# A gated unit that starts on the unnormalised state: two tiles in quarters, the deviation multiplied in at the evacuations

## The chip, the cores and the metric

The kernel runs as one program on one core of a Trainium2 chip. The metric is the device time of one execution in microseconds (us), the median of several runs. The engines run their own instruction streams and wait for each other by semaphores: TensorE (matmuls, weights 128x128, up to 512 columns a matmul, sums in eight PSUM banks), VectorE (DVE), ScalarE (ACT, with function tables), GpSimd (POOL) and SyncE, which here issues the weight loads.

## What is computed

Two transformer blocks over 256 positions and a width of 2048, all in f32. The change concerns the end of the first block, its gated unit:

```python
h = h + mixed @ w_out[l]

v = rms_norm(h, norm_ffn[l])
h = h + (jax.nn.silu(v @ w_ffn_gate[l]) * (v @ w_ffn_up[l])) @ w_ffn_down[l]

def rms_norm(x, g):
    xf = x.astype(jnp.float32)
    y = xf * lax.rsqrt(jnp.mean(xf * xf, axis=-1, keepdims=True) + RMS_EPS)
    return (y * g.astype(jnp.float32)).astype(x.dtype)
```

`w_ffn_gate` and `w_ffn_up` are 2048 x 5632. The norm's factor (one over the deviation) is one number for each position, so it is the same for all rows of a product's input and can be multiplied into the product instead.

## The kernel before

The state is kept transposed: `hT` holds 16 blocks (`KC`) of 128 features by 256 positions (`T`). An f32 product is made of three matmuls in the fast format f32r: every weight and every activation is split into a high and a low part, and high x high, high x low and low x high are summed in PSUM. A **tile** is 128 output features: 1 MB of weights, 48 matmuls of 256 columns, in two **halves** (units) of 24.

Weights come by SyncE into a ring `raw` of four tiles. `half()` exists on two engines: ScalarE copies half a tile to its high part `wh` (L1104), VectorE subtracts it from `raw` to get the low part `wl` (L1728). `wh` and `wl` have four slots, one for a half each. ScalarE may write a slot when TensorE has begun the unit behind the one that used it (semaphore `begun`, counted by `begin`). The order in each engine's stream is written out by hand. A `half()` placed before or after another step says when it can run.

`tile_T` (L510) makes one tile: 16 high x high and high x low matmuls in turn (L519, L520), then 8 with the low weights (L527), twice. It names the bank, and `reserve` lets TensorE wait until the bank's reader has freed it (`free_v6` is bank 6, read by VectorE). The names `xh`, `xl` are the split activations; in the profile both read `x`.

The steps around the change are these. `residual("out", KC)` runs 16 rows of the out projection (L578, L580, L585) into all eight banks, then VectorE adds the banks to `hT` (L1770), two banks a flag `h_ready`. ScalarE squares `hT` by quarters into `tmp` (L1181), TensorE sums the squares over partitions with 16 matmuls against ones (`sum_squares`, L607), VectorE makes the variance (L1778), ScalarE the root (L1183), VectorE the reciprocal (L1782) and four products a quarter (L1793). ScalarE splits off the high part (L1188) and VectorE the low part (L1787). `awake_till_std` runs 56 filler matmuls meanwhile (L502). Then the gated unit: for 22 turns, gate tile, up tile, gate tile, up tile, in banks 0, 4, 1, 5. ScalarE applies Silu to the gate bank (L1374), VectorE multiplies with the up bank into `hidT` (L2110).

After the norm VectorE raises `masks_free`, for which GpSimd waits to build the masks of the second block (L2667, L2627).

Of the kernel before, what the change touches and what calls it, by code (L numbers as in the profile page):

```python
# [170 lines left out]
def hold(eng, sem, value):  # L171
# [7 lines left out]
    "PE ffn": {"full_a0": 1, "begun": 8, "full_a1": 1, "full_v4": 1, "full_v5": 1},  # L179
# [7 lines left out]
    "ACT ffn": {"hi": 8, "got land0": 1, "got land1": 1, "got land2": 1, "got land3": 1, "free_a1": 1, "free_a0": 1, "gate_ready": 2},  # L187
# [7 lines left out]
    "DVE ffn": {"lo": 8, "got land0": 1, "got land1": 1, "got land2": 1, "got land3": 1, "got gate_ready": 2, "free_v4": 1, "free_v5": 1},  # L195
# [9 lines left out]
def build(nc, dram, out):  # L205
# [4 lines left out]
    with ctx:  # L210
        S = {}

        def sem(*keys):
            for key in keys:
                S[key] = ctx.enter_context(nc.semaphore(key))
# [12 lines left out]
        sem("sq_added", "gains_ready", "spread", "a_ready", "gg_in", "rs_done", "nq_ready")  # L228
# [107 lines left out]
        gt2 = at("gt2", 48, [P, 2, T])  # L336
        memT = at("memT", 32, [P, KC, T])
# [117 lines left out]
        def _(pe):  # L455
# [341 lines left out]

            residual("out", KC)
            sum_squares()
            awake_till_std(2, xkh[:, 0, :])  # L800
            normed_x()
            marks["ffn"] = k.n["full_v4"], k.n["full_v5"]
            for f in range(2):
                reserve(4 + f)
                tile_T(f, spare=None if f else 7)
                tile_T(4 + f, "v")
            with k.loop("ffn", pe, FT // 2 - 1):
                for f in range(2):
                    reserve(4 + f)
                    tile_T(f)  # L810
                    tile_T(4 + f, "v")
# [267 lines left out]
        def _(act):  # L1079
# [300 lines left out]
            with k.loop("ffn", act, FT // 2 - 1) as i:  # L1380
                unit_turn(i)
            unit_turn(FT // 2 - 1, True)
# [316 lines left out]
        def _(dve):  # L1699
# [31 lines left out]
            def split(width=HW):  # L1731

                half()
                half(width)
# [12 lines left out]
            def residual(src, name, n, more=True, between=None, early=False):  # L1747
                flag("src_ready")
                if not early:
                    for j in range(2):  # L1750
                        xsplit(src, j)
                if between is not None:
                    for j in range(n - 4):
                        split()
                        xsplit(src, 2 + j)
                        between(j)
                elif n > 4:
                    with k.loop(name, dve, n // 4 - 1) as i:
                        for j in range(4):
                            split()  # L1760
                            xsplit(src, i * 4 + (2 + j))
                for j in range(2):
                    split()
                    xsplit(src, n - 2 + j)
                if more:
                    split()
                for b in range(8):
                    take(b)
                    h = hT[:, 2 * b:2 * b + 2, :]
                    v.tensor_tensor(h, h, ps[:, b, :].rearrange("p (a t) -> p a t", a=2),  # L1770
                                    ALU.add).then_inc(*k.up(f"free_v{b}"))
                    if b % 2:
                        flag("h_ready")

# [320 lines left out]
            residual(mix1, "out", KC, early=True)  # L2095
            flag("masks_free")
            norm(hT, "norm_ffn")
            split()
            def unit_turn(i, last=False):

                for n in range(2):
                    split()
                    half()
                    if last and n == 1:
                        early_rows(hidT)
                    else:
                        half()
                    dve.wait_ge(*k.next("gate_ready"))
# [7 lines left out]
            with k.loop("ffn", dve, FT // 2 - 1) as i:  # L2116
                unit_turn(i)
            flag("early_ready")
            unit_turn(FT // 2 - 1, True)
# [682 lines left out]
```

## Time and profile before

| | |
|---|---|
| median of 3 runs (lowest, highest) | 4031.9 us (4029.94, 4036.97) |
| the profiled execution | 4031.73 us, its span 4030.0 us |
| TensorE busy, VectorE, ScalarE, GpSimd | 3969.0, 2380.7, 2064.1, 61.1 us |
| mean granted TensorE clock | 0.998 of 2.4 GHz |
| out projection ends, gated unit's first matmul | 820.78, 835.50 us |
| bytes read from HBM | 712.5 MB, 179 GB/s over the span |

All numbers of the profile come from one execution on the chip. A matmul's duration in it is longer than its share of the engine's time, because matmuls are pipelined; the distance from one start to the next is what counts. Idle times of an engine are listed with the instruction that ended them.

### The profile page before, as it was taken

How to read it: one execution, taken by the hardware profiler on the slowest of the kernel's cores; microseconds unless marked ns; L12 is line 12 of the kernel's file. 1: busy time of each engine (PE TensorE's matmuls, PEld its weight loads, DVE VectorE, ACT ScalarE, POOL GpSimd, SP SyncE). 2: the span in 40 equal slices, each digit the busy share in tenths (PEclk: the TensorE clock that was granted, in tenths of full speed). 3: DMA queues.
4: the chain of work that ended last, by engine and by line, in shares of the span. 5: the costliest groups of instructions: out<-in, count | busy, mean ns of one | idle time of the engine just before them, and what ended most of it. 6: DMA issues, size and time to landing. Idle time of an engine off the chain costs nothing.

```text
span 4030.0 us, 82891 instructions
## 1 busy us (share of the span) xinstructions
PE 3969.0 (98%) x34070; PEld 3923.8 (97%) x34070; DVE 2380.7 (59%) x3435; ACT 2064.1 (51%) x3120; POOL 61.1 (2%) x71
## 2 busy tenths in 40 slices
PE   8999999999999999999999999999999999999998
PEld 8999999999999999999999999999999999999998
DVE  7655565554444556544665666997765555555555
ACT  7555554455555444445554454447754444444443
POOL 1000000000000000000000000000000000000000
PEclk9999999999999999999999999999999999999999
DMA  5445555545555555443335544554555556665553
GB/s 209 178 158 178 179 176 186 193 157 191 194 193 193 190 195 183 168 159 125 147 137 178 178 157 147 189 190 177 183 195 197 189 194 214 217 209 193 191 195 128
DMA packets 111190, 726.10 MB, mean 180 GB/s; under 512 B 11296, under 2 KB 11424, under 8 KB 29184
## 3 DMA queue, kind: packets, MB, share of 16 engines
q1 hardware_dynamic: 105904, 701.55, 49.0%
q0 software_dynamic: 5072, 21.50, 1.7%
q8 instruction: 159, 2.61, 0.3%
q14 instruction: 55, 0.45, 0.0%
HBM read 712.52 MB, written 10.49 MB: 179 GB/s over the span
## 4 chain that ended last, share of the span: by engine, by line
PE 94%; DVE 3%; ACT 2%; issue 1%; DMA 0%; DVEq 0%; SPq 0%; ACTq 0%
PE ps L519 19%; PE ps L527 19%; PE ps L520 19%; PE ps L578 9%; PE ps L585 9%; PE ps L580 9%; PE ps L1041 1%; PE ps L651 1%; PE ps L548 1%; PE ps L549 1%; PE ps L550 1%; DVE wl L1728 1%; ACT wh L1104 1%; PE ps L607 1%; PE ps L669 1%
## 5 line engine op out<-in xcount | busy, mean ns | idle before, releaser
L1728 DVE TENSOR_TENSOR wl<-raw,wh 128x1024 fp32r<-128x1024 f32 x1328 | 1622.6, 1230 | 1446.1 <-ACT wh L1104 1440.8
L1104 ACT ACTIVATE wh<-raw 128x1024 fp32r<-128x1024 f32 x1328 | 1402.2, 1060 | 1735.5 <-PE ps L578 603.6
L519 PE MATMUL ps<-x,wh 128*128 128x256 f32 x6656 | 1582.7, 280 | 10.2 <-DVE x L1787 5.1
L520 PE MATMUL ps<-x,wh 128*128 128x256 f32 x6656 | 1567.6, 278 | 0.0
L519 PEld LDWEIGHTS ps<-x,wh 128*128 128x128 f32 x6656 | 1254.3, 188 | 19.1 <-issue 10.2
L520 PEld LDWEIGHTS ps<-x,wh 128*128 128x128 f32 x6656 | 1254.2, 188 | 0.5
L527 PE MATMUL ps<-x,wl 128*128 128x256 f32 x6656 | 899.3, 278 | 0.3 <-DVE wl L1728 0.3
L527 PEld LDWEIGHTS ps<-x,wl 128*128 128x128 f32 x6656 | 825.1, 188 | 0.5 <-DVE wl L1728 0.5
L578 PE MATMUL ps<-xkh,wh 128*128 128x256 f32 x3328 | 776.5, 276 | 3.0 <-DVE xkl L1739 1.8
L580 PE MATMUL ps<-xkl,wh 128*128 128x256 f32 x3328 | 775.7, 276 | 0.0
L578 PEld LDWEIGHTS ps<-xkh,wh 128*128 128x128 f32 x3328 | 624.8, 188 | 4.7 <-DVE xkl L1739 2.8
L580 PEld LDWEIGHTS ps<-xkl,wh 128*128 128x128 f32 x3328 | 624.8, 188 | 0.0
L585 PE MATMUL ps<-xkh,wl 128*128 128x256 f32 x3328 | 444.9, 276 | 0.0
L585 PEld LDWEIGHTS ps<-xkh,wl 128*128 128x128 f32 x3328 | 408.2, 188 | 0.0
L548 PE MATMUL ps<-y,wh 128*128 128x256 f32 x448 | 125.9, 281 | 0.0
L549 PE MATMUL ps<-y,wh 128*128 128x256 f32 x448 | 124.7, 278 | 0.0
L550 PE MATMUL ps<-y,wl 128*128 128x256 f32 x448 | 124.6, 278 | 0.0
L1635 ACT ACTIVATE oh_g<-oh_g,g_t 128x128 f32<-128x128 f32 x256 | 81.8, 390 | 9.3 <-DVE oh_g L2530 8.5
L548 PEld LDWEIGHTS ps<-y,wh 128*128 128x128 f32 x448 | 84.8, 189 | 0.7 <-issue 0.7
L550 PEld LDWEIGHTS ps<-y,wl 128*128 128x128 f32 x448 | 84.2, 188 | 0.0
L549 PEld LDWEIGHTS ps<-y,wh 128*128 128x128 f32 x448 | 84.1, 188 | 0.0
L519 PE MATMUL ps<-y,wh 128*128 128x256 f32 x192 | 48.5, 292 | 15.7 <-ACT wh L1104 15.0
(378 smaller groups left out, 2412.2 us busy)
## 6 DMA issues: line engine op xcount, KB each, us to landing
raw<-in_w_in SPq DMA_DIRECT2D x184, 1024.0 KB, 4.8
raw<-in_expert_u SPq DMA_DIRECT2D x128, 1024.0 KB, 4.8
raw<-in_expert_v SPq DMA_DIRECT2D x128, 1024.0 KB, 4.7
raw<-in_w_ffn_gate SPq DMA_DIRECT2D x44, 1024.0 KB, 4.7
raw<-in_w_ffn_up SPq DMA_DIRECT2D x44, 1024.0 KB, 4.7
raw<-in_w_ffn_down SPq DMA_DIRECT2D x44, 1024.0 KB, 4.7
raw<-in_w_out SPq DMA_DIRECT2D x32, 1024.0 KB, 4.7
raw<-in_w_branch SPq DMA_DIRECT2D x16, 1024.0 KB, 4.9
```

The lines of the kernel that those rows point to most:

```text
L519: begin(mm(o, wh[:, j, c], x_h[:, kc, :], start=kc == 0, stop=False), kc % 8 == 0)
L520: mm(o, wh[:, j, c], x_l[:, kc, :], start=False, stop=False)
L527: m = mm(o, wl[:, j, c], x_h[:, kc, :], start=False, stop=kc == KC - 1)
L548: begin(mm(o, wh[:, j, c], yh[:, y0 + n, :], start=n == 0, stop=False), kc % 8 == 0)
L549: mm(o, wh[:, j, c], yl[:, y0 + n, :], start=False, stop=False)
L550: m = mm(o, wl[:, j, c], yh[:, y0 + n, :], start=False, stop=n == nk - 1)
L578: begin(mm(o, wh[:, j, c], xkh[:, x, :], start=first and t % 2 == 0, stop=False, skip_group_check=True), t % 8 == 0)
L580: mm(o, wh[:, j, c], xkl[:, x, :], start=False, stop=False, skip_group_check=True)
L585: m = mm(o, wl[:, j, c], xkh[:, x, :], start=False, stop=last, skip_group_check=True)
L1104: f(wh[:, u % 4, 0:width], raw[:, ring, c:c + width], ACT.Copy).then_inc(*k.up("hi"))
L1635: f(o, o, ACT.Copy, scale=g_t[:, 4 * n + s:4 * n + s + 1]).then_inc(*k.up("act" if s < 3 else "lr_ready"))
L1728: v.tensor_tensor(wl[:, u % 4, 0:width], raw[:, ring, c:c + width], wh[:, u % 4, 0:width].bitcast(F32), ALU.subtract).then_inc(*k.up("lo"))
```

## The change

The gated unit takes `hT` times the gain `norm_ffn`, without the division by the deviation. ScalarE makes the high parts straight from `hT` as each quarter is ready (`raw_high`), VectorE the low parts (`raw_low`). TensorE runs the first gate tile and the first up tile together (`raw_pair`, banks 2 and 6): quarter by quarter all matmuls on high activations, then all matmuls on low activations. All four slots of `wh` and `wl` hold their weights meanwhile. The second pair of tiles follows in banks 3 and 7. VectorE adds the squares from 16 blocks down to 4, and TensorE sums them with 4 matmuls behind the fourth tile. Every evacuation then multiplies by the reciprocal `rstd`: VectorE writes the scaled gate to `gs` (Silu reads it there) and the scaled up tile to `hidT`, and multiplies the two in place. The fillers, the normalised products and their splits are gone. Loops on ScalarE and VectorE have one turn less, since the first pairs stand ahead of them.

```diff
 # TensorE
+            def raw_pair(banks, readers):
+                reserve(*banks)
+                base = k.at("begun")
+                slot = [(k.n["begun"] + u) % 4 for u in range(4)]
+                for q in range(4):
+                    pe.wait_ge(*k.next("raw_hi"))
+                    for t, b in enumerate(banks):
+                        u = 2 * t + q // 2
+                        if q % 2 == 0:
+                            pe.wait_ge(S["hi"], base + u + 1)
+                            pe.wait_ge(S["lo"], base + u + 1)
+                        for kc in range(4 * q, 4 * q + 4):
+                            c = slice(kc % 8 * P, (kc % 8 + 1) * P)
+                            begin(mm(reg(b), wh[:, slot[u], c], xh[:, kc, :], start=kc == 0, stop=False), kc == 0 and t == 0)
+                            mm(reg(b), wl[:, slot[u], c], xh[:, kc, :], start=False, stop=False)
+                for q in range(4):
+                    pe.wait_ge(*k.next("raw_lo"))
+                    for t, b in enumerate(banks):
+                        u = 2 * t + q // 2
+                        for kc in range(4 * q, 4 * q + 4):
+                            c = slice(kc % 8 * P, (kc % 8 + 1) * P)
+                            m = mm(reg(b), wh[:, slot[u], c], xl[:, kc, :], start=False, stop=kc == KC - 1)
+                            begin(m, (t, kc) in ((0, 8), (1, 12), (1, 13)))
...
             residual("out", KC)
-            sum_squares()
-            awake_till_std(2, xkh[:, 0, :])
-            normed_x()
             marks["ffn"] = k.n["full_v4"], k.n["full_v5"]
-            for f in range(2):
-                reserve(4 + f)
-                tile_T(f, spare=None if f else 7)
-                tile_T(4 + f, "v")
+            raw_pair((2, 6), "vv")
+            tile_T(3, "v", spare=0)
+            tile_T(7, "v")
+            sum_added(1, 1)
 # ScalarE
             residual(mix1, "out", KC, early=True)
-            norm(hT)
-            split(True)
+            half()
+            raw_high("norm_ffn", 0)
+            raw_high("norm_ffn", 1)
+            half()
+            raw_high("norm_ffn", 2)
+            raw_high("norm_ffn", 3)
+            for q in range(3):
+                squares(q)
+            half()
+            squares(3)
+            for _ in range(6):
+                half()
...
             def unit_turn(i, last=False):
                 for n in range(2):
-                    done(n)
-                    f(gt2[:, n, :], ps[:, n, 0:T], ACT.Silu).then_inc(*k.up(f"free_a{n}"))
-                    flag("gate_ready")
+                    half()
+                    act.wait_ge(*k.next("scaled"))
+                    half(True)
+                    silu(n)
 # VectorE
-            residual(mix1, "out", KC, early=True)
+            residual(mix1, "out", KC, early=True, halves=(3, 7))
+            for q in range(4):
+                raw_low("norm_ffn", q)
             flag("masks_free")
-            norm(hT, "norm_ffn")
-            split()
+            for _ in range(3):
+                half()
+            add_squares(8)
+            for _ in range(4):
+                half()
+            take(1)
...
             def unit_turn(i, last=False):
                 for n in range(2):
-                    split()
+                    half()
+                    scaled(n, gs[:, n, :])
+                    flag("scaled")
+                    half()
                     half()
...
+                    hid = dyn(hidT, i * 2 + (n + 2))
+                    scaled(4 + n, hid)
+                    own()
                     dve.wait_ge(*k.next("gate_ready"))
-                    take(4 + n)
-                    v.tensor_tensor(dyn(hidT, i * 2 + n), ps[:, 4 + n, 0:T], gt2[:, n, :],
-                                    ALU.mult).then_inc(*k.up(f"free_v{4 + n}"))
+                    v.tensor_tensor(hid, hid, gt2[:, n, :], ALU.mult).then_inc(*k.up("dve"))
```

TensorE before, from the end of the out projection (L585) over the sum (L607) and the fillers (L502) to the first tile (L519). What an instruction waits for stands in brackets:

```order
L585 MATMUL ps<-xkh,wl 128x256 [waits lo]
L585 MATMUL ps<-xkh,wl 128x256 x7
L607 MATMUL ps<-tmp,ones 128x256 [waits sq_ready,free_v0,free_a0]
L607 MATMUL ps<-tmp,ones 128x256 x3
L607 MATMUL ps<-tmp,ones 128x256 [waits sq_ready]
L607 MATMUL ps<-tmp,ones 128x256 x3
...
L502 MATMUL ps<-xkh 128x256 [waits free_v7,free_a7]
L502 MATMUL ps<-xkh 128x256 x7
L502 MATMUL ps<-xkh 128x256 [waits rs_std]
L502 MATMUL ps<-xkh 128x256 x47
L519 MATMUL ps<-x,wh 128x256 [waits hi,free_v0,xl_ready,free_v4,free_a4]
```

TensorE after, the same place: L586 ends the projection, L813 and L814 are high activations with high and low weights, L821 the low activations, L520 the third tile.

```order
L586 MATMUL ps<-xkh,wl 128x256 x7
L813 MATMUL ps<-x,wh 128x256 [waits raw_hi,hi,free_v6,lo,free_v2,free_a2]
L814 MATMUL ps<-x,wl 128x256
...
L813 MATMUL ps<-x,wh 128x256 [waits lo,hi]
...
L813 MATMUL ps<-x,wh 128x256 [waits raw_hi]
...
L821 MATMUL ps<-x,wh 128x256 [waits raw_lo]
L821 MATMUL ps<-x,wh 128x256 x7
L821 MATMUL ps<-x,wh 128x256 [waits raw_lo]
L821 MATMUL ps<-x,wh 128x256 x7
...
L520 MATMUL ps<-x,wh 128x256 [waits hi,free_v3,free_a3]
L521 MATMUL ps<-x,wh 128x256
```

The sum and the fillers have gone from between the projection and the tiles. The first matmul waits for six semaphores, `free_v6` among them, and the low activations stand together at the pair's end.

VectorE before, the last adds into `hT` (L1770), the flags (L1713), the variance (L1778) and the reciprocal (L1782):

```order
L1770 TENSOR_TENSOR hT<-hT,ps 128x512 [waits full_v2]
L1770 TENSOR_TENSOR hT<-hT,ps 128x512 [waits full_v3]
L1713 MEMSET small 128x1 [waits free_v3]
L1770 TENSOR_TENSOR hT<-hT,ps 128x512 [waits full_v4]
...
L1770 TENSOR_TENSOR hT<-hT,ps 128x512 [waits full_v6]
L1770 TENSOR_TENSOR hT<-hT,ps 128x512 [waits full_v7]
L1713 MEMSET small 128x1 [waits free_v7]
L1713 MEMSET small 128x1 [waits h_ready]
L1778 TENSOR_SCALAR rstd<-ps 128x256 [waits full_v0]
L1713 MEMSET small 128x1 [waits free_v0]
L1782 RECIPROCAL rstd<-rstd 128x256 [waits rs_std]
```

VectorE after. L1837 are the adds, L1795 the low parts of weight halves, L1780 the flags, L2168 the low activations; the second MEMSET shown alone is `masks_free`.

```order
L1837 TENSOR_TENSOR hT<-hT,ps 128x512 [waits full_v3]
L1780 MEMSET small 128x1 [waits free_v3]
L1795 TENSOR_TENSOR wl<-raw,wh 128x1024 [waits hi,land3]
L1837 TENSOR_TENSOR hT<-hT,ps 128x512 [waits full_v4]
L1837 TENSOR_TENSOR hT<-hT,ps 128x512 [waits full_v5]
...
L1837 TENSOR_TENSOR hT<-hT,ps 128x512 [waits full_v6]
L1837 TENSOR_TENSOR hT<-hT,ps 128x512 [waits full_v7]
L1780 MEMSET small 128x1 [waits free_v7]
L1795 TENSOR_TENSOR wl<-raw,wh 128x1024 [waits hi]
L2168 SCALAR_TENSOR_TENSOR x<-hT,par,x 128x256 [waits raw_hi]
...
L1780 MEMSET small 128x1 [waits raw_lo]
L1795 TENSOR_TENSOR wl<-raw,wh 128x1024 [waits hi,land0]
```

One weight half has moved between the adds of banks 3 and 4, another behind bank 7, and the flag `masks_free` from behind the adds to behind the 16 low activations.

## Rows read from the trace of the kernel before

**Rows 1.** The page: busy us (share of the span) xinstructions, by engine.

```profile
PE 3969.0 (98%) x34070; PEld 3923.8 (97%) x34070; DVE 2380.7 (59%) x3435; ACT 2064.1 (51%) x3120; POOL 61.1 (2%) x71
```

**Rows 2.** TensorE's waits: line <- releaser: us in total, times, longest us.

```profile
PE ps L519 <- DVE x L1787: 5.1, 5, 1.6
```

**Rows 3.** TensorE's timeline around the change: start us, us, line, operation, shapes, count.

```profile
815.33 0.28 PE L578 MATMUL ps<-xkh,wh 128*128 128x256 f32 x1
...
820.78 7.07 PE L607 MATMUL ps<-tmp,ones 128*128 128x256 f32 x32
827.50 7.45 PE L502 MATMUL ps<-xkh 128*128 128x256 f32 x56
835.50 0.36 PE L519 MATMUL ps<-x,wh 128*128 128x256 f32 x1 [0.56 <-DVE x L1787]
...
843.34 0.33 PE L496 MATMUL ps<-x,wh 128*128 128x384 f32 x1
843.51 1.07 PE L527 MATMUL ps<-x,wl 128*128 128x256 f32 x8
...
857.12 1.07 PE L527 MATMUL ps<-x,wl 128*128 128x256 f32 x8
...
859.84 1.07 PE L527 MATMUL ps<-x,wl 128*128 128x256 f32 x8
```

**Rows 4.** Two windows: length, busy us of each engine, TensorE clock, DMA share, GB/s.

```profile
823.90:835.50 11.60, 10.90 (x75) 10.06 (x74) 6.95 (x15) 4.26 (x5) 4.20 (x8) 1.00 0.00 0
870.00:1310.00 440.00, 440.00 (x3885) 440.00 (x3884) 212.26 (x204) 239.34 (x281) 0.00 (x0) 1.00 0.54 193
```

**Rows 5.** VectorE's timeline: the program's start, then around the change.

```profile
8.65 6.42 DVE L1840 SCALAR_TENSOR_TENSOR y<-hT,par,y 128x256 fp32r<-128x256 f32 x16 [8.65 <-POOL rstd L2656]
...
821.12 1.41 DVE L1770 TENSOR_TENSOR hT<-hT,ps 128x512 f32<-128x512 f32 x2
...
827.88 0.42 DVE L1778 TENSOR_SCALAR rstd<-ps 128x256 f32<-128x256 f32 x1 [4.50 <-PE ps L607]
...
834.14 1.22 DVE L1787 TENSOR_TENSOR x<-tmp,x 128x1024 fp32r<-128x1024 f32 x1
...
842.18 2.35 DVE L1728 TENSOR_TENSOR wl<-raw,wh 128x1024 fp32r<-128x1024 f32 x2
```

**Rows 6.** ScalarE's timeline: the program's start, then around the change.

```profile
7.50 6.49 ACT L1223 ACTIVATE y<-hT,par 128x256 fp32r<-128x256 f32 x16
...
815.64 1.06 ACT L1104 ACTIVATE wh<-raw 128x1024 fp32r<-128x1024 f32 x1 [1.60 <-PE ps L578]
...
821.96 1.06 ACT L1181 ACTIVATE tmp<-hT 128x1024 f32<-128x1024 f32 x1 [0.26 <-DVE small L1713]
```

**Rows 7.** VectorE: a sum of 2048 columns by shape (mean ns), and two halves at 59 us.

```profile
L1823 DVE TENSOR_TENSOR pr<-pr,rinv 128x2048 f32<-128x2048 f32 x8 | 18.3, 2292 | 0.3
...
59.21 4.55 DVE L1728 TENSOR_TENSOR wl<-raw,wh 128x1024 fp32r<-128x1024 f32 x2
```

**Rows 8.** GpSimd's timeline.

```profile
59.36 3.32 POOL L2662 TENSOR_TENSOR nq<-hT,rstd 128x1024 f32<-128x1024 f32 x1 [1.15 <-DVE x L1905]
823.46 0.56 POOL L2667 IOTA nd<- 128x512 f32 x1 [760.78 <-DVE small L1713]
824.17 0.62 POOL L2627 TENSOR_SCALAR_AFFINE_SELECT nd<-nd 128x512 f32<-128x512 f32 x1
```

**Rows 9.** TensorE at the norm of a later stage, and windows as in rows 4.

```profile
2449.07 0.36 PE L519 MATMUL ps<-x,wh 128*128 128x256 f32 x1 [0.55 <-DVE x L1787]
...
2451.83 0.58 PE L519 MATMUL ps<-x,wh 128*128 128x256 f32 x1 [1.59 <-DVE x L1787]
...
1860.00:1880.00 20.00, 19.76 (x144) 19.35 (x143) 4.40 (x7) 7.46 (x12) 0.00 (x0) 0.83 0.29 100
2440.00:2460.00 20.00, 17.71 (x129) 16.99 (x128) 17.59 (x31) 8.84 (x10) 0.00 (x0) 0.91 0.05 8
2452.00:2454.00 2.00, 2.00 (x10) 2.00 (x11) 1.96 (x6) 0.48 (x1) 0.00 (x0) 0.50 0.00 0
```

More of the change, by code:

```diff
@@ L1378, in unit_turn @@
                     done_v(4 + n, i + (marks["ffn"][n] + 1))
-            with k.loop("ffn", act, FT // 2 - 1) as i:
+            with k.loop("ffn", act, FT // 2 - 2) as i:
                 unit_turn(i)
-            unit_turn(FT // 2 - 1, True)
+            unit_turn(FT // 2 - 2, True)
             residual(hidT, "down", FT, early=True)
@@ L1745, in early_rows, with residual @@
                     xsplit(src, j)
-            def residual(src, name, n, more=True, between=None, early=False):
+            def residual(src, name, n, more=True, between=None, early=False, halves=()):
                 flag("src_ready")
@@ L2093, in _, with raw_low, add_squares, scaled @@
                 mix_in(3, q)
-            residual(mix1, "out", KC, early=True)
-            flag("masks_free")
-            norm(hT, "norm_ffn")
-            split()
+            def raw_low(gain, q):
+                dve.wait_ge(*k.next("raw_hi"))
+                for kc in range(4 * q, 4 * q + 4):
+                    v.scalar_tensor_tensor(xl[:, kc, :], hT[:, kc, :], p_col(gain, kc), xh[:, kc, :].bitcast(F32),
+                                           ALU.mult, ALU.subtract).then_inc(*k.up("raw_lo" if kc % 4 == 3 else "dve"))
+            def add_squares(count):
+                dve.wait_ge(S["sq_ready"], count)
+                step(v.tensor_tensor(tmp[:, 0:8, :], tmp[:, 0:8, :], tmp[:, 8:16, :], ALU.add))
+                v.tensor_tensor(tmp[:, 0:4, :], tmp[:, 0:4, :], tmp[:, 4:8, :], ALU.add).then_inc(*k.up("sq_sum"))
+            def scaled(b, dst):
+                take(b)
+                v.tensor_tensor(dst, ps[:, b, 0:T], rstd[:], ALU.mult).then_inc(*k.up(f"free_v{b}"))
+            residual(mix1, "out", KC, early=True, halves=(3, 7))
+            for q in range(4):
+                raw_low("norm_ffn", q)
+            flag("masks_free")
+            for _ in range(3):
[4 more added lines that the diff above has]
+            take(1)
+            v.tensor_scalar(rstd[:], ps[:, 1, 0:T], 1.0 / D, EPS, ALU.mult, ALU.add).then_inc(*k.up("free_v1"))
+            flag("rs_var")
+            dve.wait_ge(*k.next("rs_std"))
+            step(v.reciprocal(rstd[:], rstd[:]))
+            for n in range(2):
+                scaled(2 + n, gs[:, n, :])
+                flag("scaled")
+            half()
+            for n in range(2):
+                scaled(6 + n, hidT[:, n, :])
+            own()
+            for n in range(2):
+                dve.wait_ge(*k.next("gate_ready"))
+                step(v.tensor_tensor(hidT[:, n, :], hidT[:, n, :], gt2[:, n, :], ALU.mult))
             def unit_turn(i, last=False):
                 for n in range(2):
-                    split()
+                    half()
+                    scaled(n, gs[:, n, :])
+                    flag("scaled")
+                    half()
                     half()
@@ L2114, in unit_turn @@
                         half()
-            with k.loop("ffn", dve, FT // 2 - 1) as i:
+            with k.loop("ffn", dve, FT // 2 - 2) as i:
                 unit_turn(i)
             flag("early_ready")
-            unit_turn(FT // 2 - 1, True)
+            unit_turn(FT // 2 - 2, True)
             o1, o2 = PARAMS["norm_final"][0], PARAMS["norm_mix_2"][0]
```

36 lines of the change are left out of this document (31 added, 5 removed).

## The prediction, made before the changed kernel ran

> **What bounds the kernel now.** I read the page's busy times first [rows 1]: TensorE is at work for 98% of the span. So only two things can shorten the program: fewer matmuls, or less time in which TensorE has nothing useful to run. The second view is the list of TensorE's waits [rows 2]. It is short; L519 behind VectorE's L1787 (5.1 us in 5 times, none above 1.6) belongs to normalised states that are split late. The view does not show that some of TensorE's busy time is filler; that takes the order of time. The third view is therefore TensorE's timeline around the place of the change [rows 3]: the out projection ends at 820.78, 16 matmuls over the squares run to 827.5, 56 filler matmuls (L502) follow, and the first matmul of the gated unit starts at 835.50. Its first tile ends with the group that starts at 843.51, 8.9 us for what takes 5.4 in the loop, since it is starved between quarters.
>
> The gated unit's tiles are 48 matmuls each. In the loop TensorE starts a matmul each 0.1133 us: the last groups of two successive half tiles start at 857.12 and 859.84, 2.72 us apart for 24 matmuls [rows 3], and the loop window has no idle time at all [rows 4]. So a tile costs 5.44 us. In the profile before, four tiles are done at 859.84 + 8 x 0.1133 = 860.75. From 820.78 that is 39.97 us, for 4 x 5.44 = 21.76 us of real work. The other 18.2 us are the sum over squares, fillers, waits and one wide matmul. I cut the prediction to one question: when are the same four tiles (and now the sum) done after the change?
>
> **The work that remains on TensorE.** Four tiles, 21.76 us. The wide matmul of 384 columns stays, 0.17 us (843.34 to the group at 843.51 [rows 3]). The sum over squares has 4 matmuls in place of 16: L607's 16 (two records each) take 827.50 - 820.78 = 6.72 us, 0.42 each [rows 3], so 4 take 1.68 us. Together 23.6 us. The 56 fillers are gone. What is left is the waiting.
>
> **The wait at the start.** The first new matmul waits for raw_hi, and also for free_v6 and free_v2, since both banks are reserved before either is written (TensorE's order in the section on the change). Bank 6 is emptied late. Before, VectorE's adds end at 822.53 for bank 6 (the pair that starts at 821.12 and lasts 1.41) [rows 5]. The change puts one weight half on VectorE between banks 3 and 4; two such halves take 2.35 us, the pitch is 1.16 [rows 5]. So bank 6 is free at 823.69, and TensorE starts 0.14 to 0.2 us later (L519 starts at 835.50, L1787 before it ends at 835.36 [rows 3, 5]): 823.85. The first high activations do not decide: ScalarE copies them from 819.4 at 0.40 each (16 in 6.49 us [rows 6]), so quarter 0 is there at 821.1 and quarter 1 at 822.7. The wait is 823.85 - 820.78 = 3.1 us.
>
> **The pair by quarters, step by step.** ScalarE's fourth half waits for that first matmul (begun): it starts 0.3 us after it (815.64 against 815.33 [rows 3, 6]), 824.15 to 825.2. Then quarters 2 and 3 of the high part, 1.6 us each: 826.9 and 828.5. TensorE needs quarter 2 after 32 matmuls, at 827.5, and quarter 3 at 829.3. Both are covered, by 0.6 and 0.8 us. VectorE does its fourth half 825.3 to 826.5, then the low parts at 0.40 each (16 in 6.42 us [rows 5]): 828.2, 829.8, 831.4, 833.0. The low pass is last; TensorE comes to it at 831.1 and to its last quarter at 833.8. Covered, the tightest by 0.8 us. So the pair runs without a gap, 96 x 0.1133 = 10.9 us, to 834.7. If one of the covers is gone, its lateness counts once and in full.
>
> **Tiles 3 and 4 and the sum.** Slots of the weight ring come free only in the low pass, the first at 832.9. ScalarE has by then squared three quarters (1.06 each [rows 6]) from 828.5 to 831.7, writes the next half by 834.3, and TensorE wants it at 834.7. VectorE finishes its halves at about 835.7, 837.6 and 838.7; each is wanted 1.8 us after its half tile starts, so 836.5, 839.4 and 842.1. Then it adds squares: 2048 columns as L1823's 2.29 and 1024 as L1787's 1.22 [rows 5, 7], to 842.4, and the next half to 843.6, wanted at 844.9. TensorE reaches the sum at 834.7 + 10.9 + 0.17 = 845.8, the squares have been there for 3.4 us, and the four tiles and the sum are done at 847.5. Gain: 860.75 - 847.5 = 13.3 us.
>
> **What is moved beside VectorE.** The flag masks_free now stands behind the low parts, at 833.1, and GpSimd's mask building (four generators of 0.56 us and four selections of 0.62 us, 4.7 us from 823.46 [rows 8]) moves from a stretch where VectorE was idle to one where it makes weight halves. What that costs is not shown for these instructions. The bounds: nothing, as for L1778's 0.42 us, which ran beside them at 827.88 [rows 5, 8]; or what one tensor multiply of GpSimd did at 59.36, where two weight halves took 4.55 us in place of 2.35 [rows 7, 8]. Doubling VectorE for 5 us, or for up to 10 us if GpSimd is slowed too, makes the half behind the squares late by 1 to 4 us. I take 0: each GpSimd instruction is shorter than a weight half, as L1778's case is nearer, and the margins above are 0.8 to 3.5 us. The Trainium skill, page "SBUF — State Buffer", section "Who interferes with whom", has VectorE operations with two SBUF inputs contend only with GpSimd operations that read SBUF, the later one blocked for the whole instruction. By it only the selections count, each delays a half by at most its own 0.62 us and the sum stays; the 4.55 us row agrees with blocking by a reader, and no row shows the case of a generator that only writes.
>
> **The rest costs nothing.** Behind the sum stand variance, root, reciprocal and products. Before, all from the variance at 827.88 to the first split state at 835.36 took 7.5 us [rows 5], more than what is left of it now; TensorE has halves for three units made in advance and needs bank 0 again only after four more tiles, 21.8 us. In the loop each of the 42 tile pairs gets two more products on VectorE (0.42 each), and the weight half that waited for the gate tile now waits for the first of them: it is ready 2.0 us after the tile, wanted after 5.44 + 2.72 = 8.2. VectorE is busy 212 of 440 us there, ScalarE 239 [rows 4]; the extra products and a flag each add 38. SyncE's loads follow the same halves, and from 823.9 to 835.5 the rings stood full, with no transfer at all [rows 4].
>
> **The clock.** A price that the sum lacks. TensorE now stands still for 3.1 us in one piece. The longest idle time of this stage before was 1.6 us [rows 2], and the granted clock stayed at 1.00 [rows 4]. But at 2450, the norm of a later stage, idle times of 0.55 and 1.59 us ended in a clock of 0.50, 1.2 GHz; over the 20 us it granted 0.91, so 0.09 x 20 = 1.8 us were lost [rows 9]. At 1860 it granted 0.83, 3.4 us lost. So idle times half as long cost the clock in one of two like places. With 3.1 us in one piece I think a fall likelier than not, and take 1.7 us for it, near the place that is alike; the ends are 0 and 3.4. The page "TensorE: Matmul & The Clock Gate" of the Trainium skill, section "HAM oscillation — how this bites in real kernels", says that a wait of TensorE between bursts can make the next burst start cold; by it the fall is the rule here.
>
> **Sum.** The profiled execution took 4031.7 us (span 4030.0), the runs' median is 4031.9. 4031.9 - 13.3 = 4018.6, with the clock's fall 4020.3.
>
> **Rivals.**
> - No fall of the clock: 4018.6. For it: the stage before went through at full clock. Against: 3.1 us is twice what was there. 0.25.
> - Starved halves: contention with GpSimd, or quarters that come a bit later than I place them, cost 2 to 4 us more: 4022 to 4024.5. For it: five steps with margins of 0.4 to 0.8 us stand in a row. Against: lateness in the pair does not add up, as each quarter is made at its own pitch, faster than TensorE uses it (1.6 against 1.8 us). 0.15.
> - The early start is not had at all, because another wait takes its place in full (the last h add, or the low quarters behind a late half): TensorE would start at 828 or so, gain 9: 4023 to 4025, at the edge of what can be told. 0.05.
> - Slower than before: the product before the gate's function stands in the loop on the path of the weight halves. Price 0.42 + 0.06 + some 0.24 us of waits, 0.72 for each of 42 gate tiles, 30 us: 4048.8. It decides only when the half behind the product comes more than 8.2 us after the gate tile; I count 2.0. 0.04.
> - The forecast, gain 13.3 less 1.7: 0.51.
>
> **Numbers.** 4020.3. The likeliest cases span 4017 to 4023. The runs of the kernel before lie between 4029.9 and 4037.0, so that a median of few runs moves by a us or two by itself, and later stages can meet or miss a fall of the clock (1.7 to 3.4 us): 4015.5 to 4026.5 for 8 in 10. A difference of 0.2% is 8.1 us, about what a measurement of this kernel can tell from none; it is reached below 4023.8. The forecast, the first rival and half of the second and third make 0.86 for faster, 0.84 with that wandering taken off; same 0.12, slower 0.04.
>
> **What the profile after would show.** The first matmul of the pair at about 823.85, 3.1 us behind the last of the out projection, released by VectorE's add into hT (not by ScalarE's copy). No wait above 0.3 us until the sum. A half tile every 2.72 us (or, for a stretch of 3 to 7 us, matmuls 0.21 apart with clock 0.5). The sum of 4 done about 26.7 us behind the out projection, 28.4 with the fall. The loop without idle time. I am wrong if TensorE is released by something other than bank 6, if a gap of over 1 us stands inside the first four tiles, or if the loop's pitch is above 21.76 us a turn.

## The result, and where the time went

| | before | after |
|---|---|---|
| median of 20 runs (lowest, highest) | 4031.55 us (4029.93, 4036.97) | 4037.43 us (4033.40, 4041.26) |
| ratio of the two, 95% interval | | 1.0015 [1.0008, 1.0022] |
| span of the profiled execution | 4030.0 us | 4037.7 us |

The kernel became 5.9 us slower. The interval of the ratio lies above 1, so the loss is clear of the noise, though it is only 0.15%. I had forecast some 11 us faster, with 4 in 100 for slower. Against [rows 1], the page of the changed kernel has TensorE busier by 7.1 us, although it runs 80 records fewer.

```profile
PE 3976.1 (98%) x33990; PEld 3931.9 (97%) x33990; DVE 2418.5 (60%) x3561; ACT 2004.9 (50%) x3047; POOL 63.3 (2%) x71
```

The new wait at the start is the one of the forecast, in place and size, and the starving between quarters is gone. These are TensorE's waits after (line <- releaser: us in total, times, longest); the second row is what is left, in the norms of later stages, of the 5.1 us of [rows 2].

```profile
PE ps L813 <- DVE hT L1837: 3.1, 1, 3.1
PE ps L520 <- DVE x L1856: 3.0, 3, 1.6
```

TensorE's timeline after, to be laid beside [rows 3]. L813 is the pair's high pass, L821 its low pass, L497 the matmul of 384 columns, L528 the low weights of a half tile, L832 the sum, L520 the first tile of the loop.

```profile
819.57 1.07 PE L586 MATMUL ps<-xkh,wl 128*128 128x256 f32 x8
823.75 0.35 PE L813 MATMUL ps<-x,wh 128*128 128x256 f32 x1 [3.11 <-DVE hT L1837]
...
831.36 3.93 PE L821 MATMUL ps<-x,wh 128*128 128x256 f32 x32
...
837.01 1.10 PE L528 MATMUL ps<-x,wl 128*128 128x256 f32 x8
...
839.84 0.34 PE L497 MATMUL ps<-x,wh 128*128 128x384 f32 x1
...
842.76 1.07 PE L528 MATMUL ps<-x,wl 128*128 128x256 f32 x8
...
845.48 1.08 PE L528 MATMUL ps<-x,wl 128*128 128x256 f32 x8
846.39 1.89 PE L832 MATMUL ps<-tmp,ones 128*128 128x256 f32 x8
847.93 0.47 PE L520 MATMUL ps<-x,wh 128*128 128x256 f32 x1
...
903.71 1.11 PE L528 MATMUL ps<-x,wl 128*128 128x256 f32 x8
...
906.54 1.10 PE L528 MATMUL ps<-x,wl 128*128 128x256 f32 x8
```

The projection ends at 820.48 (819.57 + 8 x 0.1133). The four tiles and the sum are done at 847.93, 27.45 us later, where the kernel before took 39.97 for its four tiles: 12.5 us are gained, of 13.3 forecast. But look at the distances between the L528 groups. From 842.76 to 845.48 they are 2.72 us, as in [rows 3]. In the loop, from 903.71 to 906.54, they are 2.83 us for the same 24 matmuls. A matmul each 0.1178 us has taken the place of one each 0.1134, and no wait is shown. The windows after, the first to be laid beside [rows 4], say how long it lasts (length, busy us and instructions of PE, PEld, DVE, ACT, POOL, clock, DMA share, GB/s):

```profile
870.00:1310.00 440.00, 440.00 (x3738) 440.00 (x3737) 238.91 (x313) 176.99 (x195) 0.00 (x0) 1.00 0.52 186
1320.00:1560.00 240.00, 239.84 (x2114) 239.63 (x2114) 126.51 (x139) 106.30 (x131) 0.00 (x0) 1.00 0.55 192
```

TensorE is busy all of the loop's 440 us in both kernels at a granted clock of 1.00, but runs 3738 matmuls there, not 3885: 850 in 100 us, not 883. In the down projection behind it the rate is back. So a view of busy times, waits and clock shows nothing; only the number of matmuls in a window does.

The account, all from the two profiled executions. From the projection's end to the end of the fourth tile (and the sum): 27.45 - 39.97 = -12.5 us. From there to the first matmul of the down projection, 84 tiles: 1323.33 - 847.93 = 475.4 after, 1318.13 - 860.75 = 457.4 before: +18.0. Behind it, to the span's end: 2714.4 against 2711.9, +2.5. Of that, 1.7 us come in and behind a late part of the attention: the same matmul starts at 2161.24 after and at 2155.20 before, 6.0 us apart, and from 2160 to 2220 TensorE runs 494 matmuls against 516. Ahead of it -0.3. Together +7.7, the difference of the spans.

**Two rhythms.** TensorE's matmuls of 256 columns come either each 0.1134 us or each 0.1178 us, often hundreds in a row. Below, these are the dense and the loose rhythm (in the expectations, the fast and the slow rate). The kernel before has the loose one too; I had not looked for it. One stretch is the mix stage, from 614.8 us until 737.6, where it ends at a 384-column matmul in the out projection's first row. 100 us of it, before:

```profile
620.00:720.00 100.00, 100.00 (x851) 100.00 (x851) 56.08 (x69) 43.16 (x53) 0.00 (x0) 1.00 0.51 182
```

In the changed kernel the pair starts loose, behind its wait of 3.1 us: of the 64 matmuls from 823.75 to 831.36 the first takes 0.19 us and the others 0.1178 each. It stays so up to L497 at 839.84, and is dense behind it. The sum follows at 846.39, the loop starts loose at 847.93 and stays so to the loop's end. The first matmul of the down projection, at 1323.33 behind a wait of 0.16 us for VectorE's xkl, begins a dense stretch again, 4 us ahead of that stage's own 384-column matmul; so that one is not what ended the loose rhythm. A wait need not end it either: in number 7 below the same wait (0.17 us) left the stream loose, up to that stage's 384-column matmul at 1328.56. 84 tiles x 48 x 0.0044 us = 17.7 us, which is the 18.0 of the account. What I had to show was that this rhythm, and not the loop's new work, is what costs, and what sets it.

### The profile page after: what moved, and what is told of

Same layout as the page of the kernel before. It is cut to its first block, busy times and chain, and to the rows that moved or that the text cites. A ratio compares the mean times of both kernels' runs of the same rounds, so it can differ in the third digit from the quotient of the medians.

```text
span 4037.7 us, 82811 instructions
## 1 busy us (share of the span) xinstructions
PE 3976.1 (98%) x33990; PEld 3931.9 (97%) x33990; DVE 2418.5 (60%) x3561; ACT 2004.9 (50%) x3047; POOL 63.3 (2%) x71
## 4 chain that ended last, share of the span: by engine, by line
PE 95%; DVE 3%; ACT 1%; issue 1%; DMA 0%; DVEq 0%; SPq 0%; ACTq 0%
PE ps L520 19%; PE ps L528 19%; PE ps L521 19%; PE ps L579 9%; PE ps L586 9%; PE ps L581 9%; PE ps L1075 1%; PE ps L652 1%; PE ps L549 1%; PE ps L550 1%; PE ps L551 1%; PE ps L670 1%; ACT wh L1138 1%; DVE wl L1795 1%; PE ps L608 1%
## 5 line engine op out<-in xcount | busy, mean ns | idle before, releaser
L1795 DVE TENSOR_TENSOR wl<-raw,wh 128x1024 fp32r<-128x1024 f32 x1328 | 1622.1, 1229 | 1396.2 <-ACT wh L1138 1390.6
L520 PE MATMUL ps<-x,wh 128*128 128x256 f32 x6624 | 1586.4, 281 | 8.1 <-DVE x L1856 3.0
L520 PEld LDWEIGHTS ps<-x,wh 128*128 128x128 f32 x6624 | 1249.9, 189 | 16.7 <-issue 9.2
L528 PE MATMUL ps<-x,wl 128*128 128x256 f32 x6624 | 901.0, 279 | 0.3 <-DVE wl L1795 0.3
L528 PEld LDWEIGHTS ps<-x,wl 128*128 128x128 f32 x6624 | 826.8, 189 | 0.5 <-DVE wl L1795 0.5
L586 PE MATMUL ps<-xkh,wl 128*128 128x256 f32 x3328 | 445.0, 276 | 0.0
L586 PEld LDWEIGHTS ps<-xkh,wl 128*128 128x128 f32 x3328 | 408.2, 188 | 0.0
L520 PE MATMUL ps<-y,wh 128*128 128x256 f32 x192 | 48.3, 291 | 16.0 <-DVE y L1909 15.3
```

What stands on the lines that cost most here:

```text
L520: begin(mm(o, wh[:, j, c], x_h[:, kc, :], start=kc == 0, stop=False), kc % 8 == 0)
L528: m = mm(o, wl[:, j, c], x_h[:, kc, :], start=False, stop=kc == KC - 1)
L586: m = mm(o, wl[:, j, c], xkh[:, x, :], start=False, stop=last, skip_group_check=True)
L1795: v.tensor_tensor(wl[:, u % 4, 0:width], raw[:, ring, c:c + width], wh[:, u % 4, 0:width].bitcast(F32), ALU.subtract).then_inc(*k.up("lo"))
```

## The experiments

Times are medians, the ratio is to the kernel before, measured beside each experiment on the same chip. The chip matters: there the kernel before had medians of 4030.4 us (numbers 1 to 4), 4033.6 (5 to 8) and 4034.1 (9 to 11), so forecasts in us that start from 4037.4 come out 2 to 3 us low in the later ones. The loop is always read in the window 870 to 1310 us.

**1. One 384-column matmul directly behind the sum.**

```diff
                 m.then_inc(*k.up(f"full_v{b}"))
+                wide((k.n["begun"] - 1) % 4, 0)
```

> Theory P (pitch): the changed kernel loses its gain because TensorE leaves the sum's four f32 matmuls in a slow rhythm, one matmul each 0.1178 us instead of 0.1134, and keeps it through the whole loop of the gated unit until the 384-column matmul of the down projection at 1323 us. One 384-column matmul right behind the sum, the only edit, restores the rhythm: the loop shows 885 matmuls per 100 us instead of 851, and 475 us x 3.8% = 18 us come back: about 4019.5 us (4017 to 4022). Rival E (evacuations): VectorE's additional products slow TensorE's reads or the banks' release in the loop; the edit leaves them all, so the loop stays at 851 per 100 us and the time at 4037.5. Rival D (data): activations without the deviation have other sizes and draw another clock; also 4037.5.

Measured: 4037.98 us, ratio 1.0018 [1.0009, 1.0027]. A miss. TensorE's timeline of this run at the sum, and two of its windows:

```profile
848.77 1.89 PE L832 MATMUL ps<-tmp,ones 128*128 128x256 f32 x8
850.31 0.53 PE L497 MATMUL ps<-x,wh 128*128 128x384 f32 x1
850.67 0.28 PE L520 MATMUL ps<-x,wh 128*128 128x256 f32 x1
...
826.00:828.00 2.00, 2.00 (x12) 2.00 (x11) 2.00 (x4) 2.00 (x7) 0.00 (x0) 0.50 0.00 0
870.00:1310.00 440.00, 440.00 (x3738) 440.00 (x3737) 239.31 (x313) 176.59 (x194) 0.00 (x0) 1.00 0.53 186
```

The matmul took 0.36 us to the next one's start instead of the 0.17 it takes inside a tile, and the loop stayed loose. Taken alone this spoke for the rivals. A side result: after its wait the clock fell in this execution (0.50 in the window shown), and the pair came out of the fall in the dense rhythm at 829.9. The sum came upon a dense stream, without idle time ahead of it, and left a loose one.

**2. The kernel before without its 384-column matmul.**

```diff
-                tile_T(f, spare=None if f else 7)
+                tile_T(f)
```

> The mirror image in the kernel before: its only edit takes out the one 384-column matmul of the first gate tile; nothing of the evacuations or the data changes. Theory P: the slow rhythm that the first tile shows from 835.5 goes on to 1318 us, 483 us x 3.8% = 18.5 us more: about 4050 us (4047 to 4053), with 851 matmuls per 100 us in the loop. Rivals E and D: 4031.5, loop at 883.

Measured: 4030.51 us, ratio 1.0005 [0.9995, 1.0014]. A miss, as I had expected about 4050. But one of the 11 runs took 4051.0 us. The profiled one went through a fall of the clock in the first tile, and its loop was dense:

```profile
838.00:840.00 2.00, 2.00 (x11) 2.00 (x11) 1.96 (x5) 1.34 (x2) 0.00 (x0) 0.50 0.00 0
870.00:1310.00 440.00, 440.00 (x3885) 440.00 (x3884) 211.56 (x205) 239.98 (x280) 0.00 (x0) 1.00 0.55 193
```

So that matmul wasn't needed in ten runs of eleven. The profile of the kernel before, which has it, shows why it may not be. The first tile is loose behind the sum and turns dense at a break of 0.1 us within it, 0.8 us ahead of the 384-column matmul at 843.34:

```profile
842.31 0.39 PE L519 MATMUL ps<-x,wh 128*128 128x256 f32 x1
842.54 0.28 PE L520 MATMUL ps<-x,wh 128*128 128x256 f32 x1
```

From 842.54 to 843.34 seven matmuls start, 0.114 us apart; from 841.39 to 842.09 six, 0.117 apart. The eleventh run of this experiment is 20 us longer, about what I forecast for all. It was not profiled, so that its rhythm was the loose one is not shown.

**3. The sum ahead of the fourth tile, the 384-column matmul in the fourth.**

```diff
-            tile_T(3, "v", spare=0)
-            tile_T(7, "v")
+            tile_T(3, "v")
             sum_added(1, 1)
+            tile_T(7, "v", spare=0)
```

> The changed kernel with the sum moved ahead of the fourth tile, and its 384-column matmul moved from the third tile into the fourth, so behind the sum. No matmul is added or taken away. Theory P: the loop runs at 885 per 100 us; TensorE waits about 2.5 us for the added squares, so 4037.4 - 18 + 2.5 + 0.4 = 4022 us (4019.5 to 4024.5). If what restores the rhythm is not that matmul but something else of the place, or by E and D: 4037 to 4041.

Measured: 4023.36 us, ratio 0.9981 [0.9972, 0.9990]. TensorE's timeline and windows:

```profile
843.64 3.60 PE L832 MATMUL ps<-tmp,ones 128*128 128x256 f32 x8 [2.76 <-DVE tmp L2175]
...
851.62 0.33 PE L497 MATMUL ps<-x,wh 128*128 128x384 f32 x1
...
844.00:846.00 2.00, 2.00 (x6) 1.55 (x6) 1.77 (x2) 0.00 (x0) 0.00 (x0) 0.50 0.09 12
870.00:1310.00 440.00, 439.82 (x3881) 439.62 (x3880) 248.71 (x325) 185.15 (x206) 0.00 (x0) 1.00 0.55 192
```

A hit: the same matmuls in another order, all the changed loop's products on VectorE (248.7 us busy, against 212.3 in [rows 4]), the same raw activations, and the rate is that of the kernel before. Rivals E and D fall with this run. The stall ahead of the sum was 2.76 us (VectorE's L2175) and brought a fall of the clock. In this profile the tile was dense before L497, so the run by itself doesn't show that L497 is what does it.

**4. The sum as f32r.**

```diff
-    m = mm(reg(b), ones[:], tmp[:, kc, :], start=kc == 0, stop=kc == 3)
+    m = mm(reg(b), ones_r[:], tmp_r[:, kc, :], start=kc == 0, stop=kc == 3)
...
# VectorE
-                v.tensor_tensor(tmp[:, 0:4, :], tmp[:, 0:4, :], tmp[:, 4:8, :], ALU.add).then_inc(*k.up("sq_sum"))
+                step(v.tensor_copy(ones_r[:], ones[:]))
+                v.tensor_tensor(tmp_r[:], tmp[:, 0:4, :], tmp[:, 4:8, :], ALU.add).then_inc(*k.up("sq_sum"))
```

> The changed kernel with the sum over squares in the fast format: VectorE writes the added squares and a copy of the ones as f32r, and the four matmuls of the sum run as one pass each. No 384-column matmul is added. It asks what drops the rhythm. Theory P1: the two-pass f32 matmuls do; then the rhythm stays fast, and the sum takes 0.5 us instead of 1.5: about 4018.5. Theory P2: any break in the stream (a wait for a semaphore, other operands) drops it; then the loop stays at 851 and the time at about 4036.5. E and D: 4036.5.

Measured: 4035.38 us, ratio 1.0012 [1.0002, 1.0021]. Loose, from the sum's first matmul on (845.19; the four took 0.47 us), so the plain f32 format of the sum, whose four matmuls take 1.54 us in the changed kernel, is not what loosens the rhythm.

```profile
870.00:1310.00 440.00, 440.00 (x3738) 440.00 (x3737) 239.37 (x313) 176.84 (x195) 0.00 (x0) 1.00 0.53 185
```

**5. A 384-column matmul in the first gate tile of every turn.**

```diff
-                    tile_T(f, "v")
+                    tile_T(f, "v", spare=None if f else 2)
```

> The changed kernel with a 384-column matmul in the first gate tile of every loop turn, between high and low weights of its second half, the sum left where it is. Theory P with one correction from the runs so far (directly behind the sum that matmul does not help, inside a running tile it does): the slow rhythm ends in the first turn, the loop runs at 0.1134 us a matmul apart from 21 x 0.17 = 3.6 us for the added matmuls: 4037.4 - 18 + 3.6 = 4023 us (4021 to 4025). If the order of work of the changed loop itself keeps the rhythm slow: 4037.4 + 3.6 = 4041.

Measured: 4026.84 us against 4033.58 before on that chip, ratio 0.9981 [0.9972, 0.9990].

```profile
870.00:1310.00 440.00, 439.73 (x3869) 439.53 (x3868) 247.28 (x325) 183.85 (x203) 0.00 (x0) 1.00 0.54 192
```

The loop began loose (847.9) and was dense from 852.7 on, behind the first of these matmuls at 852.50. This is the cleanest sight of the restoring: the place of the sum, the loop and its work are as in the changed kernel. The time is above the 4021 to 4025 that I had written, on a chip on which the kernel before took 2 us more.

**6. The sum inside the fourth tile, and 7. the same with the 384-column matmul left ahead of it.**

```diff
-            tile_T(3, "v", spare=0)
-            tile_T(7, "v")
-            sum_added(1, 1)
+            tile_T(3, "v")
+            tile_T(7, "v", spare=0, mid=lambda: sum_added(1, 1))
# 7 instead
+            tile_T(3, "v", spare=0)
+            tile_T(7, "v", mid=lambda: sum_added(1, 1))
```

> The changed kernel with the sum between the two halves of the fourth tile and its one 384-column matmul in that tile's second half (taken from the third tile). No work is added. Theory P: the added squares are ready when TensorE comes there (VectorE ends them at 843.3, TensorE begins that half at 843.7), so no stall, and the loop is fast: 4037.4 - 18 = 4019.5 us (4017 to 4022). Evacuations or data as the cause: 4037.4.

> As the run before it in this list, with the sum between the halves of the fourth tile, but the 384-column matmul stays in the third tile, ahead of the sum. Theory P: the sum drops the rhythm and nothing restores it: 4037 us, 851 matmuls per 100 us in the loop. Rival Q (a break inside a tile is harmless, only one at the boundary between the tiles and the loop costs): 4019.5, 885 per 100 us.

Measured, 6: 4022.20 us, ratio 0.9970 [0.9959, 0.9980]. 7: 4041.71 us, ratio 1.0019 [1.0010, 1.0028]. By their edits the two differ in the tile that holds one matmul of 0.17 us; by their times, in 19.5 us. Number 6 from the half tile ahead of the sum to its 384-column matmul, and its loop:

```profile
841.78 1.07 PE L530 MATMUL ps<-x,wl 128*128 128x256 f32 x8
842.89 1.97 PE L834 MATMUL ps<-tmp,ones 128*128 128x256 f32 x8
...
845.51 0.28 PE L523 MATMUL ps<-x,wh 128*128 128x256 f32 x1
...
846.53 0.33 PE L497 MATMUL ps<-x,wh 128*128 128x384 f32 x1
...
870.00:1310.00 440.00, 439.73 (x3879) 439.54 (x3879) 250.76 (x329) 183.46 (x203) 0.00 (x0) 1.00 0.55 193
```

The same place in number 7, and its loop:

```profile
843.53 1.08 PE L530 MATMUL ps<-x,wl 128*128 128x256 f32 x8
844.45 1.89 PE L834 MATMUL ps<-tmp,ones 128*128 128x256 f32 x8
...
846.29 0.28 PE L523 MATMUL ps<-x,wh 128*128 128x256 f32 x1
...
870.00:1310.00 440.00, 440.00 (x3739) 440.00 (x3738) 239.73 (x313) 176.40 (x195) 0.00 (x0) 1.00 0.53 186
```

Rival Q falls: in number 7 the sum stands inside the tile, and the loop is loose. Number 6 is 11.4 us under the kernel before: it is what I had forecast for the changed kernel.

But number 6 does not show its 384-column matmul restoring anything. From 845.51 to 846.53, ahead of that matmul, nine matmuls start 0.1133 us apart, at a clock of 1.00: the stream was dense already. In number 7 ten start from 846.29 to 847.47, 0.118 apart. What also differs in the profiles is the arrival at the sum. In number 6 TensorE was ready for it at 842.69 (841.78 + 8 x 0.1134) and started it at 842.89, as VectorE's added squares were there only at 842.75; in number 7 it ran on into the sum. The same holds for number 3, which waited 2.76 us ahead of its sum. So all five sums of this kind that a dense stream ran into without idle time left it loose (the changed kernel, numbers 1, 4, 5 and 7), and those behind a wait did not (3, 6 and, below, 10). Whether it is the wait or the moved matmul that parts the times of 6 and 7, no run tells.

**8. Four fillers for the sum, and 9. the same with the sum's wait.**

```diff
-    m = mm(reg(b), ones[:], tmp[:, kc, :], start=kc == 0, stop=kc == 3)
+    m = mm(reg(b), wh[:, (k.n["begun"] - 1) % 4, kc * P:(kc + 1) * P], xh[:, kc, :], start=kc == 0, stop=kc == 3)
# 8 only
-                pe.wait_ge(S["sq_sum"], count)
```

> Leaves out the deviation (it is taken as 1): in place of the sum stand four fast-format matmuls with weights and activations of the last tile, and no wait for the squares. It asks whether the sum's wait and operands drop the rhythm, or four more matmuls at that place do. If the wait and the operands do: 885 per 100 us and about 4018.5 us. If any four matmuls do (as the sum in the fast format hints, which went slow at its own first matmul): 851 and 4036.

> Leaves out the deviation (taken as 1), as the run with fillers before: four fast-format matmuls with the last tile's own operands stand in place of the sum, but now with the sum's wait for the added squares ahead of them, which have long been ready. If the wait drops the rhythm: 851 matmuls per 100 us in the loop and about 4 to 6 us over the kernel before. If the sum's operands do (the ones as weights, the squares as moving data): 885 and some 13 us under the kernel before.

Both leave out the deviation, so what they compute is not the gated unit's result. Measured, 8: 4019.87 us, ratio 0.9965 [0.9951, 0.9980]; 9: 4020.16 us, ratio 0.9965 [0.9951, 0.9980], from four runs each. The loops of 8 and 9:

```profile
870.00:1310.00 440.00, 439.73 (x3879) 439.53 (x3879) 251.40 (x329) 182.82 (x202) 0.00 (x0) 1.00 0.55 193
```

```profile
870.00:1310.00 440.00, 439.73 (x3878) 439.53 (x3877) 250.33 (x329) 183.56 (x203) 0.00 (x0) 1.00 0.55 193
```

Both dense, with no 384-column matmul behind. TensorE had no idle time at number 9's wait, since the squares had long been added. So neither that semaphore nor four more matmuls loosen the rhythm; with number 4 it is the sum's operands, the ones and the squares, that do, in either format, where the stream runs into them without idle time.

**10. The best version.** Number 6, and two more 384-column matmuls, one in the pair's first quarter and one in the first tile of the mix stage. The edit in the mix stage:

```diff
-                    fill_gate(4 * q + t)
+                    if q + t:
+                        fill_gate(4 * q + t)
+                    else:
+                        tile_T(1, spare=2)
```

> The best version: the sum between the halves of the fourth tile with its 384-column matmul behind it, and two more such matmuls: in the first quarter of the pair, and in the first gate tile of the mix stage, which runs slow from 614.8 to 739.2 us in the kernel before. Theory P: 124 us x 3.8% = 4.7 us less 0.17 in the mix stage, and up to 0.6 us in the pair, on top of the 11 us that the moved sum gave under the kernel before: 16 us under it (14.5 to 17.5), ratio 0.996. If the rhythm is not a state that one matmul sets: 11 us, as without them.

Measured: 4015.44 us against 4034.09, ratio 0.9956 [0.9942, 0.9970], 18.7 us faster than the kernel before; the most I had written was 17.5. The mix stage was loose up to its new matmul at 623.25 and dense behind it. The sum waited 0.2 us and left the stream dense, as in number 6.

```profile
620.00:720.00 100.00, 100.00 (x883) 100.00 (x882) 56.86 (x67) 44.29 (x55) 0.00 (x0) 1.00 0.54 190
870.00:1310.00 440.00, 439.73 (x3878) 439.53 (x3877) 251.18 (x330) 185.13 (x205) 0.00 (x0) 1.00 0.54 192
```

**11. The kernel before with the mix stage's alone.** The edit shown under number 10, and no other.

> The kernel before with one 384-column matmul added, in the first gate tile of the mix stage, and no other edit. Theory P: that stage's slow 124 us become fast, 4.7 - 0.17 = 4.5 us under the kernel before, ratio 0.9989; in its windows 885 matmuls per 100 us instead of 851. Rivals E and D have nothing here that could change: no difference, or 0.2 us more.

Measured: 4029.46 us, ratio 0.9988 [0.9979, 0.9997], 4.6 us faster for one matmul more.

```profile
620.00:720.00 100.00, 100.00 (x882) 100.00 (x882) 57.43 (x70) 45.31 (x55) 0.00 (x0) 1.00 0.55 191
```

This is the second place at which adding one matmul changed the rate of all behind it (loose up to 624.64), in a stage that the change never touched.

**All profiles together.** In the 13 profiled executions, those of both kernels and of these eleven, a loose stream came upon a 384-column matmul 29 times, and each time it was dense behind it. No unbroken stream of 256-column matmuls went from loose to dense by itself. Behind a wait it can be either, from the same instructions: behind the pair's wait of 3.1 us it was loose in the changed kernel and in numbers 7 and 9, and dense in numbers 1, 3, 4, 5, 6 and 8 (number 10 has a 384-column matmul there).

## Why the prediction was wrong

**The start, right.** TensorE waited 3.11 us for bank 6 (forecast 3.1) and started at 823.75 (823.85), released by VectorE's add. The pair ran without a gap.

**Four tiles and the sum, nearly right.** 27.45 us against 26.7 forecast. The sum took 1.54 us (1.68). The other 0.9 us: the loose rhythm of the pair and of the third tile up to 839.84 costs 0.6 us (136 matmuls, 0.0044 each), the pair starts 0.2 us later behind the projection's end than forecast, and its first matmul takes 0.1 us more than the rest.

**GpSimd beside VectorE, priced at 0, and it cost TensorE nothing.** The forecast had a rival for it. VectorE's rows after, the adds and then the halves and the squares beside GpSimd's mask building:

```profile
821.44 2.00 DVE L1837 TENSOR_TENSOR hT<-hT,ps 128x512 f32<-128x512 f32 x3
...
836.62 2.78 DVE L1795 TENSOR_TENSOR wl<-raw,wh 128x1024 fp32r<-128x1024 f32 x2 [0.61 <-ACT wh L1138]
839.32 2.70 DVE L2174 TENSOR_TENSOR tmp<-tmp 128x2048 f32<-128x2048 f32 x1
842.05 1.22 DVE L2175 TENSOR_TENSOR tmp<-tmp 128x1024 f32<-128x1024 f32 x1
```

Two halves took 2.78 us in place of 2.35 and the addition of 2048 columns 2.70 in place of 2.29, so about 0.4 us each; 842.05 + 1.22 is 0.9 us later than forecast, and still 3.1 us ahead of TensorE at the sum.

**The clock, right in size, but it falls in some executions only.** In the changed kernel's profile it didn't fall at the wait; in the profile of experiment 1 it did, at the same wait, down to 0.50 for some 6 us. Ten of the profiled kernels have this wait, and the clock fell behind it in four (numbers 1, 5, 7 and 8). From 822 to 832 us the mean granted clock was 0.83 in three of them, so 1.7 us were lost, the term of the forecast; in number 1 it was 0.66, so 3.4. That the fall is the rule here, as the prediction has it, these ten don't bear out. The runs of the changed kernel spread over 7.9 us, and the longer ones have the lower mean clock: three at 0.996 took 4041.0 to 4041.3 us, eight at 0.998 or more had a median of 4035.2. It is a matter of 1.7 to 3.4 us and not of the 18 of the loop.

**The loop, the step that failed.** The forecast says "In the loop TensorE starts a matmul each 0.1133 us" and "So a tile costs 5.44 us", and takes that over for the tiles after. It was a reading of one rhythm, not a property of the tile. After, the loop's tiles cost 475.4 / 84 = 5.66 us, or 22.6 us a turn; a pitch above 21.76 was one of the signs of being wrong that the prediction named. The section "The rest costs nothing" looked at waits and at other engines' load, where indeed nothing is: no idle time, clock 1.00. The term mis-sized is the loop's pitch, put at no change; it cost 18.0 us against the 12.5 gained at the start. The rival for a slower kernel blamed a wait in the loop, so it had the side right and the cause wrong. Experiments 3 and 6 refute it: the loop with the same products runs at the old rate.

**What I could have seen.** The diff moved the one 384-column matmul from behind the sum to ahead of it. I priced it as 0.17 us and never asked what it was there for. That move alone is not the cause, as number 2 shows; the cause is a sum that a dense stream runs into, with nothing behind it that restores. And the trace of before had the loose rhythm in about a fifth of its time, 614.8 to 737.6 in one piece.

**What stays open.** What the two rhythms are inside TensorE is not shown. Nor is why the 384-column matmul restores the dense one inside a stream (numbers 5, 7, 10's mix stage, 11) but not directly behind the sum (number 1), or which of the sum's two operands loosens it. Nor what decides which rhythm follows a wait, as at the pair's start, at 1323.33 and behind the sums that came after a wait. A run of number 6 without its 384-column matmul, or with its sum a few tenths of a us later, would say what its gain hangs on.

## What to carry to other kernels

When TensorE is the bound, compare the number of matmuls per microsecond in each stage, in both kernels, before pricing anything else; a rate of 4% less over a loop costs more than most stalls and leaves no idle time. Treat an odd instruction that seems to do nothing as something to be explained before the change moves it. Where matmuls with other operands (sums against ones) break into a long stream, look at the rate behind them; if it fell, a wider matmul some way behind them, inside the stream and not directly behind them, brought it back here (number 5; the third tile of number 7).

## What the runs showed of the hardware

- Two steady rates of f32r matmuls with 128x128 weights and 256 columns, 0.1134 and 0.1178 us each at a granted clock of 1.00 without idle time, one of them kept over 475 us and across a loop's 21 turns.
- A matmul of 384 columns inside a stream turned loose to dense, at a cost of 0.17 us (839.84 in the changed kernel, 852.50 in number 5, 840.61 in number 7; 29 times of 29 in all profiles). Directly behind the sum it did not (850.31 in number 1).
- A fall of the clock does not set the rhythm. Behind it the stream was dense at 829.9 in number 1, 841 in number 2 and 847 in number 3, and loose at 827.05 in number 7 and at 2455 in the kernel before.
- TensorE's wait of 3.1 us ended at a clock of 1.00 in six profiles and at 0.50 in four, from the same instructions up to it.
- GpSimd and VectorE slowed each other. GpSimd's selections take 0.62 us on an idle VectorE before; beside the weight halves one took 1.49 and the last two 2.72 together:

```profile
834.78 1.22 DVE L1795 TENSOR_TENSOR wl<-raw,wh 128x1024 fp32r<-128x1024 f32 x1 [1.86 <-ACT wh L1138]
835.00 1.49 POOL L2739 TENSOR_SCALAR_AFFINE_SELECT nd<-nd 128x512 f32<-128x512 f32 x1
...
837.16 2.72 POOL L2739 TENSOR_SCALAR_AFFINE_SELECT nd<-nd 128x512 f32<-128x512 f32 x2
```

The Trainium skill, page "SBUF — State Buffer", section "Who interferes with whom", has the one that comes second blocked for the whole instruction. The selection at 835.00 came second and ended 0.49 us behind the half of 834.78, which agrees with it.
